# Expert biases of a mixture-of-experts layer: a 6-row selector matmul per pair, or four 32-row groups loaded once

## The reference, cut to what matters

```python
def body(e, acc):
    gu = t @ w_gu[e] + b_gu[e]          # 1024 x 2048, bias of 2048
    g, u = jnp.split(gu, 2, axis=-1)
    ...
    y = hdn @ w_dn[e] + b_dn[e]         # 1024 x 1024, bias of 1024
    return acc + comb[:, e][:, None] * y
```

## Time and profile before

| | us |
|---|---|
| device time, median of 3 runs | 1383.08 |
| lowest and highest of them | 1382.1, 1387.19 |
| span of the profiled execution, first to last instruction | 1385.6 |
| front part, up to the first L1065 | 397.3 |
| a body of the loop (645.3 to 768.0) | 122.7 |
| last use of a weight chunk begins | 1371.1 |

### The profile page before, as it was taken

How to read it: one execution, slowest core, us unless ns; L and a number is a source line. 1 busy time by engine, 2 the same in 40 slices (tenths; PEclk the granted TensorE clock), 3 DMA queues, 4 the chain that set the end, 5 groups by cost and what they waited for, 6 DMA issues and landing times.

```text
span 1385.6 us, 14006 instructions
## 1 busy us (share of the span) xinstructions
PE 1331.6 (96%) x5590; PEld 621.6 (45%) x5590; DVE 416.1 (30%) x798; ACT 161.9 (12%) x289; POOL 12.4 (1%) x26
## 2 busy tenths in 40 slices
PE   5999999999989999999999999999999999999997
PEld 1786458888443333333333333433343333333332
DVE  4079993893421021121112022110201031021103
ACT  3202005130120010001001000010100011010000
POOL 0000010000000000000000000000000000000000
PEclk9999999999979999999999999999999999999999
DMA  9945133797468999999999999999999899999991
GB/s 360 386 168 177 61 126 107 284 359 287 186 284 369 361 422 421 402 407 421 420 379 424 420 403 401 422 420 366 420 421 414 355 422 421 395 407 420 421 388 57
DMA packets 85249, 477.57 MB, mean 345 GB/s; under 512 B 3952, under 2 KB 4624, under 8 KB 36064
## 3 DMA queue, kind: packets, MB, share of 16 engines
q1 hardware_dynamic: 84160, 473.48, 84.9%
q0 software_dynamic: 1056, 3.64, 0.8%
HBM read 476.06 MB, written 1.05 MB: 344 GB/s over the span
## 4 chain that ended last, share of the span: by engine, by line
PE 89%; DVE 4%; ACT 3%; issue 2%; DMA 1%; SPq 0%; DVEq 0%; ACTq 0%
PE bank L1065 31%; PE bank L1113 17%; PE bank L788 10%; PE bank L1127 5%; PE bank L987 5%; PE bank L999 4%; PE bank L954 3%; PE bank L797 3%; PE bank L974 2%; ACT area_sb L1327 2%; DVE area_sb L1855 2%; PE bank L717 1%; PE bank L836 1%; PE bank L827 1%; DVE area_sb L1864 1%
## 5 line engine op out<-in xcount | busy, mean ns | idle before, releaser
L1065 PE MATMUL bank<-ring_sb,area_sb 128*64 128x512 f32 x1536 | 352.6, 609 | 11.5 <-ACT area_sb L1327 11.5
L1065 PEld LDWEIGHTS bank<-ring_sb,area_sb 128*64 128x64 f32 x1536 | 107.1, 140 | 226.5 <-issue 216.8
L788 PE MATMUL bank<-area_3h_sb,ring_sb 128*128 128x256 f32 x704 | 153.9, 379 | 0.0
L788 PEld LDWEIGHTS bank<-area_3h_sb,ring_sb 128*128 128x128 f32 x704 | 133.1, 190 | 19.6 <-issue 1.1
L1113 PE MATMUL bank<-ring_sb,area_sb 128*64 128x512 f32 x640 | 140.5, 593 | 0.0
L1879 DVE TENSOR_TENSOR area_sb<-area_sb,bank 128x512 f32<-128x512 f32 x64 | 44.1, 688 | 284.2 <-PE bank L1127 284.2
L1855 DVE TENSOR_SCALAR area_sb<-bank 128x512 f32<-128x512 f32 x32 | 22.0, 688 | 316.4 <-PE bank L1065 316.4
L1065 PE MATMUL bank<-area_sb 128*64 128x512 f32 x512 | 114.7, 595 | 0.0
L1327 ACT ACTIVATE area_sb<-bank 128x512 f32<-128x512 f32 (+1 forms) x80 | 42.3, 549 | 525.5 <-PE bank L987 441.9
L1886 DVE TENSOR_TENSOR area_sb<-bank,area_sb 128x512 f32<-128x512 f32 x32 | 22.1, 692 | 215.0 <-PE bank L1113 215.0
L1113 PEld LDWEIGHTS bank<-ring_sb,area_sb 128*64 128x64 f32 x640 | 45.3, 137 | 87.8 <-issue 86.8
(11 more groups left out here) (246 smaller groups left out, 851.1 us busy)
## 6 DMA issues: line engine op xcount, KB each, us to landing
ring_sb<-w_gu SPq DMA_DIRECT2D x96, 2048.0 KB, 15.7
ring_sb<-w_down SPq DMA_DIRECT2D x40, 2048.0 KB, 14.6
area_sb<-w_gu SPq DMA_DIRECT2D x32, 2048.0 KB, 17.1
area_sb<-w_down SPq DMA_DIRECT2D x16, 2048.0 KB, 9.2
ring_sb<-w_in SPq DMA_DIRECT2D x14, 2048.0 KB, 11.9
ring_sb<-w_ada SPq DMA_DIRECT2D x12, 2048.0 KB, 10.5
area_3h_sb<-w_down SPq DMA_DIRECT2D x8, 2048.0 KB, 24.5
ring_sb<-w_branch SPq DMA_DIRECT2D x3, 2048.0 KB, 11.2
```

What stands on the lines that cost most here:

```text
L788: ins = pe.matmul(b[:, m * SEQ:(m + 1) * SEQ], w[:, k, (m0 + m) * P:(m0 + m + 1) * P], hT[:, k, :], start=k == 0, stop=k == KT - 1)
L1065: ins = pe.matmul(bank[n][r, :], xT[:, k, r], w[:, e, n * 512:(n + 1) * 512], start=False, stop=k == KT - 1, skip_group_check=True)
```

## The change

The biases of all 32 experts are loaded once, in four bands of 32 partitions: band n of `bias_gu` holds quarter n of every expert's gate-and-up bias (512 floats), bands 0 and 1 of `bias_down` the two halves of the down bias. A selector `bias_sel` of 128 rows, one for each pair of a body, is written by DVE per pair: row p has ones in the columns of the expert whose number is p modulo 32. Each bias matmul takes one band of 32 rows of both. The selector of 6 rows, its making on POOL and the per-pair DMAs and their waits on SP go; six DMAs on POOL come. The gain of the second norm moves to another area, since the biases stay in its old one's neighbourhood for the whole loop.

```diff
-            def load_bias(b, j):
-                e0 = j * 4 + 2 * b
-                sp.dma_start(bias[:, b, :], a["b_experts"][bass.ds(e0, 2), :]
-                             .rearrange("e (g m) -> (e g) m", g=3)).then_inc(bias_landed[b], 16)
...
-                    if n == BIAS_AT and not last:
-
-                        sp.wait_ge(y_done, i * 4 + 1)
-                        load_bias(0, j + 1)
...
-                    sp.wait_ge(y_done, i * 4 + 3)
-                    load_bias(1, j + 1)
...
+            for g in range(4):
+                pool.dma_start(bias_gu[32 * g:32 * g + 32, :], a["b_experts"][:, g * 512:(g + 1) * 512])\
+                    .then_inc(bias_landed, 16)
+            for g in range(2):
+                pool.dma_start(bias_down[32 * g:32 * g + 32, :], a["b_experts"][:, (4 + g) * 512:(5 + g) * 512])\
+                    .then_inc(bias_landed, 16)
...
-            def gate_bias(i, b):
-
-                pe.wait_ge(bias_landed[b], i * 16 + 16)
+            def select_rows(b, n):
+
+                return bias_sel[32 * n:32 * n + 32, b, :, :].rearrange("p e s -> p (e s)")
+
+            def gate_bias(i, p, b):
+
+                pe.wait_ge(bias_sel_made, 2 * i + p + b + 1)
                 pe.wait_ge(gate_up_read, i * 4 + 4 + 2 * b)
                 for n in range(4):
-                    c = (n % 2) * 512
-                    pe.matmul(bank[n][:, :], row_sel[:, n // 2, :], bias[:, b, c:c + 512],
+                    pe.matmul(bank[n][:, :], select_rows(b, n), bias_gu[32 * n:32 * n + 32, :],
                               start=True, stop=False, skip_group_check=True)
...
                 for n in range(2):
-                    ins = pe.matmul(bank[4 + n][:, :], row_sel[:, 2, :], bias[:, b, n * 512:(n + 1) * 512],
-                                    start=True, stop=False, skip_group_check=True)
+                    pe.matmul(bank[4 + n][:, :], select_rows(b, n), bias_down[32 * n:32 * n + 32, :],
+                              start=True, stop=False, skip_group_check=True)
...
+            def bias_rows(b, expert):
+
+                dve.tensor_copy(bias_sel[:, b, :, :],
+                                tile_sums[:, bass.ds(expert, 2)].rearrange("p (e o) -> p e o", o=1)
+                                .to_broadcast([P, 2, SLOTS])).then_inc(bias_sel_made, 1)
...
                         members(j + 1, i + p + 2)
+                        bias_rows(0, j * 4 + 4)
+                    else:
+
+                        bias_rows(1, j * 4 + 2)
                     y_out(i, b)
```

More of the change, by code:

```diff
@@ L52 @@
 SLOT_OF = list(range(MOE_SLOTS)) + list(range(7)) + list(range(8))
-BIAS_AT = 20
 FAR = 4096.0
@@ L234, in build_layer @@
         before = sb("before", [P, P])
-        row_sel = sb("row_sel", [6, 3, P])
         flag = sb("flag", [P, 1], I32)
@@ L300, in build_layer @@
         y_s = view(area_2, 3072, [D])
-        bias = area_6[0:6, 0:2 * FF].rearrange("p (b m) -> p b m", b=2)
+        bias_gu, bias_down = area_6[:, 0:512], area_6[0:64, 512:1024]
+        bias_sel = view(area_6, 1024, [2, 2, SLOTS])
         moe_slots = [ring[:, (NF + n) % WEIGHT_SLOTS, :] for n in range(WEIGHT_SLOTS)]
@@ L308, in build_layer @@
         turned = view(area_8, 512, [SEQ])
-        norm2_gain = view(area_6, 2048, [D])
+        norm2_gain = view(area_3, 2048, [D])
         squares = view(area_2, 0, [W])
@@ L338, in build_layer @@
         logit = view(area_2, 1600, [TT, EXPERTS])
-        tile_sum = view(area_5, TT * D, [EXPERTS])
+        tile_sums = view(area_5, TT * D, [EXPERTS + 4])
+        tile_sum = tile_sums[:, 0:EXPERTS]
         expert_no = sb("expert_no", [P, EXPERTS])
@@ L420, in build_layer @@
         misc_out = {"act": sem("misc_out_act"), "dve": sem("misc_out_dve")}
-        bias_landed = [sem(f"bias_landed{b}") for b in range(2)]
+        bias_landed = sem("bias_landed")
+        tile_sum_made = sem("tile_sum_made")
+        bias_sel_made = sem("bias_sel_made")
         gate_min = sem("gate_min")
@@ L641, in _ @@
             step(pool.memset(before[:, :], 1.0))
-            step(pool.memset(row_sel[:, :, :], 0.0))
             step.wait()
@@ L648, in _ @@
                                     base=0, pattern=[[1, P]], channel_multiplier=-1))
[L650 to L653, removed]
             step(pool.iota(iota[:, :], pattern=[[1, SLOTS]], base=0, channel_multiplier=0,
@@ L1005, in router @@
                     wait_emptied(pe, before_in_bank(n, len(JOBS)))
-                gate_bias(0, 0)
+                pe.wait_ge(bias_landed, 16 * 6)
+                gate_bias(0, 0, 0)
                 for t in range(TT):
@@ L1029, in router @@
                 wait_emptied(pe, "partial")
+                pe.wait_ge(tile_sum_made, 1)
                 for t in range(TT):
@@ L1137, in body @@
                     if b == 0:
-                        gate_bias(i, 1)
+                        gate_bias(i, p, 1)
                     elif not last:
-                        gate_bias(i + 1, 0)
+                        gate_bias(i + 1, p, 0)
                 for n in range(4):
@@ L1145, in one_pass @@
                 if not first:
-                    gate_bias(p * BODIES, 0)
+                    gate_bias(p * BODIES, p, 0)
                 with pe.Fori(0, BODIES - 1) as j:
@@ L1751, in _ @@
                     step.wait()
-            step(dve.tensor_reduce(tile_sum, ident[:, :].rearrange("p (g e) -> p e g", e=EXPERTS),
-                                   AX_X, ALU.add))
+            dve.tensor_reduce(tile_sum, ident[:, :].rearrange("p (g e) -> p e g", e=EXPERTS),
+                              AX_X, ALU.add).then_inc(tile_sum_made, 1)
+            def bias_rows(b, expert):
+                dve.tensor_copy(bias_sel[:, b, :, :],
+                                tile_sums[:, bass.ds(expert, 2)].rearrange("p (e o) -> p e o", o=1)
+                                .to_broadcast([P, 2, SLOTS])).then_inc(bias_sel_made, 1)
+            dve.wait_ge(tile_sum_made, 1)
+            bias_rows(0, 0)
             wait_emptied(dve, "adab7")
@@ L1913, in one_pass @@
                 members(0, p * (BODIES + 1) + 1)
+                if not first:
+                    bias_rows(0, 0)
                 if first:
```

## The result

The changed kernel takes 1339.0 us (median of 4 runs, 1337.8 to 1340.2) where the kernel before takes 1383.9 on the same chips: a ratio of 0.9677, 95% interval 0.9659 to 0.9694. The profiled execution of the changed kernel took 1337.8 us, of which its span, first to last instruction, is 1336.0.

A forecast was written before the change was run, and what follows sets the result against it. PE was taken as the bound, with weights close behind. PE's body would fall from 122.7 to 111.4 us, weights' to 119.3; along the loads 1385.6 - 36.6 - 15 - 1 = 1333 us span, hence 1331 us, range 1323 to 1350.

The forecast's parts named there:

- The second limit: Expert loop: the weight stream moves at most 422 GB/s, 119.3 us a body, so it becomes the bound after 3.4 us.
- Rival D: Weight loads: a full stream gets only 410 GB/s, so only the 15 us in hand are won, 1368 us; chance 0.06.
- C: Bias matmuls on PE: the bands don't run at once, PE and clock stay as before, 1383 us; chance 0.05.
- Gate bias, 1.12 us: Gate bias on PE: four bands run at once, 1.12 us instead of 3.69, saving 2.57 each, 15 times in the loop.
- B: Bias matmuls on PE: bands taken strictly in order, a gate bias at 2.4 us; chance 0.06.
- Down bias, a saving of 0.86: Down bias on PE: two bands run at once, saving 0.86 us each, 16 times in the loop.
- the forecast does not hang on the clock: Whole kernel: if no fall of the clock went, PE alone would still give 1385.6 - 52.3 = 1333.3 us, the same.
- The clock: PE behind bias matmuls: most falls to half clock go, between 0 and 4.4 us a body, taken as 4.4.
- From span to time: Final conversion: span 1333 us; the same loss from 1385.6, taken off the runs' median 1383.1, gives 1330.5, said as 1331.
- Rival E: PE in the loop: new waits for weights drop the clock, making it slower, 1437 us at twelve falls a body; chance 0.03.
- Costs counted at nothing: POOL's six bias loads and DVE's selector copy cost 0; removing SP's sixteen loads gains nothing, up to 1 us.

The follow-up runs named there:

- the full-array kernel: Every bias matmul over all 128 rows of selector and biases, one after the other, against the changed kernel (values wrong): 1343.2 us, ratio 0.971 to the kernel before.
- the kernel with the bias in the gap: Changed kernel with the next pair's gate biases moved into the wait before the first down matmul: 1334.8 us, ratio 0.9652 to the kernel before; again 1335.4.
- the one-band kernel: Changed kernel with every bias matmul taken from band 0, so none run at once (values wrong): 1369.8 us, ratio 0.9886 to the kernel before.

## Why the prediction was right, and where it wasn't

The forecast was 1331 us, range 1323 to 1350; 1339.0 came.

*The second limit.* Right, and it is what makes the number. The stream was predicted to move 422 GB/s without a pause and moves 421 from 448 to 1321; the last chunk was to be used as it lands, and is (1321.35 and 1321.39). Counted in span, the forecast was 1333 and 1336.0 came. SP's waits for L1065, now L1056, shrank from 554.6 to 379.1 us. Rival D (410 in a full stream) is out, and C (no overlap) too.

*Gate bias, 1.12 us.* It takes 1.14; the first records of its four matmuls start at 738.157, 738.163, 738.170 and 738.177. That four bands of 32 rows run at once as two of 64 do held; B, bands in order, would have taken 2.4.

*Down bias, a saving of 0.86.* This term is wrong: it was worth nothing. I priced the matmul and didn't ask what ended the wait behind it. The chain stands in the timeline of all engines. Of the changed kernel, around the down bias:

```profile
720.67 0.69 DVE L1868 SCALAR_TENSOR_TENSOR area_sb<-area_sb 128x512 f32<-128x512 f32 x1
721.28 0.68 DVE L1855 TENSOR_SCALAR area_sb<-bank 128x512 f32<-128x512 f32 x1
...
721.42 0.74 PE L1080 MATMUL bank<-ident_sb,area_sb 128*128 128x128 f32 x4 [0.23 <-DVE area_sb L1868]
...
722.00 0.63 ACT L1327 ACTIVATE area_sb<-area_sb 128x512 f32<-128x512 f32 x1 [2.18 <-DVE area_sb L1855]
722.54 0.85 ACT L1318 ACTIVATE area_sb<-bank 128x256 f32<-128x256 f32 x2
...
723.44 1.51 PE L1104 MATMUL bank<-area_sb 128*64 128x512 f32 x6 [1.28 <-ACT area_sb L1318]
```

And the same place of the kernel before:

```profile
740.03 0.75 PE L1089 MATMUL bank<-ident_sb,area_sb 128*128 128x128 f32 x4
740.05 0.63 ACT L1336 ACTIVATE area_sb<-area_sb 128x512 f32<-128x512 f32 x1 [2.17 <-DVE area_sb L1855]
740.59 0.85 ACT L1327 ACTIVATE area_sb<-bank 128x256 f32<-128x256 f32 x2
```

ACT copies the transposed hidden rows (L1318 now, L1327 before) only behind its sigmoid of the second half, which waits for DVE's L1855. The sigmoid starts 1.93 us after the down bias in both kernels (722.00 - 720.07; 740.05 - 738.12), the copy behind it 2.47 us after (722.54 and 740.59), and the transposes were over or nearly over by then. So PE's end of the bias was never the last to come. A body by PE is therefore 113.3 us and not 111.4, and without this term the sentence "the forecast does not hang on the clock" falls as well: with all falls kept, PE alone would end at 1385.6 - 15 x 2.57 = 1347 in span, above the stream's 1336. So 11 us hung on the falls going: enough of them went, as the prediction expected, but its claim that the number did not need them was wrong.

*The clock.* The direction was right. The price of all falls was nearly right, 4.7 us a body instead of 4.4 (the full-array kernel). But the term took all of them as gone, and only those behind the gate bias went; behind the down bias 9 are left where there were 8. The prediction looked at the 6 rows alone and not at the wait behind L1096, although one of its three rows of a fall, L1113 at 801.69, stands behind an L1096 and that wait. Bodies of up to 116.9 us instead of 111.4 used up the weights in hand in the sixth body, where PE first waits at 1061.86, and not in the second or third. It cost nothing in the end, because the stream was full all along: the kernel with the bias in the gap, without a fall in the loop, takes as long from the second row on.

*From span to time.* With 5 us the largest part of the miss of 8. I took a loss of 52 us of span off the median of the runs, 1383.1. But time is span plus 1.8 us (1337.8 and 1336.0), and the profiled execution of before, with its span of 1385.6, was thus a run of about 1387, the slowest shown. The span fell by 49.6, the medians by 44.9. Span plus what lies around it, 1333 + 1.8 = 1335, would have been the honest number.

*Rival E.* Waits for weights came, in the body from 1093 on about 6 us (119.3 - 113.3), and the clock there stayed at 0.99. With the bias in the gap PE waited from the fourth body on, and the mean clock was 0.994. Waits of up to 1.3 us before a chunk brought no fall at all there.

*Costs counted at nothing.* POOL's six loads, DVE's copy (0.22 us, not above the 0.29 taken as bound) and SP's 16 loads: none shows; for SP's loads the one-band kernel is the evidence.

One thing stays open: how many falls come in an execution. The same kernel in one band had between 63 and 91 us at half clock, and the changed kernel 10.2 or 27.3 us of it before its loop was under way.

## What to carry to other kernels

Before you price a shorter instruction, look one wait further: if the next wait is for another engine's chain, the saving turns into waiting. When two resources lie within 3% of each other, work out the second's floor from its unbroken rate; the end was right here although two terms of the first resource's sum were not. When a group of matmuls uses few rows, look at the granted clock behind it: filling the rows can be worth as much as running them at once. And when two kernels differ by a few us, look in the traces where the difference arises before you credit the edit.

## What the runs showed of the hardware

Float32 matmuls on four bands of 32 rows and into four banks run at once: 8 records in 1.14 us against 3.69 one after the other. TensorE's clock fell to its lower level behind matmuls whose records stood back to back but used 6 rows of 128 (15 times in the loop behind a gate bias); the same number of records over 128 rows left it at 1.00, and the gate bias in four bands at once brought no fall either. A down bias over 32 rows, in one band or two, followed by waits of PE for other engines, was still followed by a fall 9 times in the loop; over 128 rows, or with the gate bias in the wait, by none. The mean clock over the execution was 0.958 to 0.962 with 6 rows, 0.967 to 0.977 with 32 rows one at a time, 0.993 with 128. One microsecond at half clock cost this kernel some 0.43 us where PE was the bound. The stream of weights kept 421 to 422 GB/s for 873 us.
